# A third gate buffer and a new order of work around the state chunks of a delta-rule stage

## The chip, the cores and the metric

The kernel runs on one core of a Trainium2 chip. The metric is the device time of one execution in microseconds. Everything is float32; large matrix products are made of three products of rounded parts (high x high, high x low, low x high).

## What is computed

One decoder layer over 256 tokens of 2048 features: a half-step SwiGLU, a mixing layer (8 heads of latent attention beside 16 heads of an RWKV-7 delta rule), its output projection, a second half-step SwiGLU, and a gated per-layer embedding. The change concerns the delta rule alone:

```python
def step(state, inp):                  # for each of 16 heads, state 64 x 64
    r_t, w_t, k_t, v_t, kk_t, a_t = inp
    sa = jnp.einsum('bhvk,bhk->bhv', state, -kk_t)
    state = (state * w_t[:, :, None, :]
             + sa[..., None] * (kk_t * a_t)[:, :, None, :]
             + v_t[..., None] * k_t[:, :, None, :])
    return state, jnp.einsum('bhvk,bhk->bhv', state, r_t)
init = jnp.zeros((B, H, N, N))
...
o = (o - mu) * lax.rsqrt(var + GN_EPS)            # per head
o = o * ln_x_w + ln_x_b
o = (o + bonus) * g                                # bonus = sum(r*k*r_k) * v
```

## The kernel before

The 16 heads go through in four groups of four heads (`GROUPS`, r = 0 to 3), and a group's 256 tokens in four chunks of 64 (`NCHUNK`); two chunks make a tile of 128 tokens (t = 0, 1). For each group there are four steps.

1. **Front** (`front`, `with_decay`, on VectorE): keys, unit keys `kk`, learned keys `bb`, decayed copies `alpha`, `R_`, `B_`, `Kd`, the bonus. ScalarE makes the gates (`act_gates`), the last of them the output gate `gg`, from products that TensorE makes part by part (`pe_gates`). All of this is done for group r + 1 while group r is worked on. `gg` and `bonus` have two buffers each, used in turn.
2. **Scores and inverse** (`pe_scores`, `pe_inverse`, `inverse`): TensorE multiplies the turned keys, and a unit triangular matrix is inverted for each of 8 systems (4 heads x 2 tiles) in six levels. The first needs no products, the other five are n = 0 to 4. A level n is two rounds of products with a ScalarE copy into `Q` between and a VectorE copy into `XT` or `X` after, in halves of four systems. Levels 0 and 1 (`EARLY`) stand behind the scores, 2 to 4 (`LATER`) at the start of the group's turn. Level 3 is followed by AK times v (`pe_y`), which ScalarE copies into `Y` (`act_y`).
3. **State** (`pe_state`, `act_state`, `state`): products of alpha with X (copied to `W1T` by VectorE), then X with Y (copied to `U` by ScalarE), and a recurrence over the four chunks c. In chunk c, W1T times the state S is subtracted from U (VectorE, L1688), the queries read S (L1409), and Kd times v plus B_ times U (L1415, L1421) give the next S (VectorE, L1693 or L1698), with the decayed old state `SP` from ScalarE. S starts as a cleared buffer, which chunk 0 reads too. After chunk 1 TensorE turns (transposes) the next group's alpha into bank 3 (`turn`), after chunk 3 R_, B_ and Kd.
4. **Finish** (`out_centre`, `out_spread` on VectorE, `finish`, `gate_ahead` on GpSimd): centre, normalise, gate and add the bonus into `og`. TensorE transposes `og` (`pe_out`, into bank 1), ScalarE copies it to `xT_hi` (`act_out`), VectorE writes the rounding rest to `xT_lo` (`out_lo`). These three stand behind the inverse of the next group and ahead of its state step.

Each engine has its own queue, in the order of the program text; semaphores tie them together. `act_gates` waits, before it overwrites a `gg` buffer, for `o_ready` of the group that used it two groups before (L1488 to L1490). On ScalarE's queue that copy stands ahead of `Y` and of the copies of level 4. GpSimd's order is written out: `gate_ahead(0)`, `finish(0)`, `gate_ahead(1)`, `finish(1)` and so on. VectorE's work for the next group stands between the levels: key (L1569, L1580) behind level 2; own key and read (L1584, L1585, L1594) behind level 3; unit key and learned (L1588, L1589, L1569, L1592) behind level 4; read gain and read sum (L1569, L1598) ahead of chunk 0's S.

Of the kernel before, what the change touches and what calls it, by code (L numbers as in the profile page):

```python
# [16 lines left out]
P = 128  # L17
# [14 lines left out]
CHUNK = 64  # L32
# [85 lines left out]
def hybrid_layer(nc, table, w, out):  # L118
    where = constant_table()[1]
    ctx = ExitStack()  # L120
    with ctx:
# [1020 lines left out]
        def pool_rwkv(pool):  # L1142
# [5 lines left out]
            def gate_ahead(r):  # L1148

                b, k = bonus[:, r % 2, :, :], gg[:, r % 2, :, :]  # L1150
# [7 lines left out]
            def finish(r):  # L1158
# [5 lines left out]
                tt(og[:, :, :], oo[:, :, :], gg[:, r % 2, :, :], ALU.mult)  # L1164
# [40 lines left out]
        def sp_rwkv(sp):  # L1205
# [78 lines left out]
        def turn(pe, r, k):  # L1284
# [4 lines left out]
            if k == 3 and r:  # L1289
                pe.wait_ge(rs_copied, 2 * r)  # L1290
# [84 lines left out]
        def pe_state(pe, r, nxt):  # L1375

            pe.wait_ge(up_ready, 11 * r + 11)
# [61 lines left out]
        def pe_out(pe, r):  # L1439
            pe.wait_ge(o_ready, r + 1)  # L1440
            pe.wait_ge(ak_ready, 2 * min(r + 2, GROUPS))
            for pr in range(2):
                for t in range(TT):
                    ins = nc.tensor.transpose(PS[:, 1, (2 * pr + t) * P:(2 * pr + t + 1) * P], og[:, t, pr * P:(pr + 1) * P], ident)
# [7 lines left out]
        def pe_rwkv(pe):  # L1452
# [20 lines left out]
        def act_gates(act, r, part):  # L1473
# [22 lines left out]
        def act_scores(act, r, before):  # L1496
# [4 lines left out]
            act.wait_ge(bonus_ready, r + 1)  # L1501
# [513 lines left out]
```

## Time and profile before

| | |
|---|---|
| median of 3 runs | 2067.5 us (2067.19 to 2068.78) |
| the profiled execution's own time | 2067.66 us |
| its span | 2065.8 us |
| TensorE (PE) busy | 2024.1 us, 98% |
| VectorE (DVE) busy | 1155.3 us, 56% |
| ScalarE (ACT) busy | 859.6 us, 42% |
| GpSimd (POOL) busy | 148.0 us, 7% |
| DMA moved | 373.62 MB, 181 GB/s on the mean |

The delta-rule stage takes from about 997 us to 1139.5 us of the span. Times in the trace are microseconds from the span's start; a row has the start, the duration, the engine, the line and the operation, and in square brackets the time for which the engine had been idle and what released it. A busy TensorE is not TensorE at its peak. PEclk is the clock granted to TensorE, in parts of the full 2.4 GHz.

### The profile page before, as it was taken

Reading aid. Unit: us, or ns where it says so; the run is one execution under the profiler, and the core shown is the slowest. Engines: PE = TensorE matmul, PEld = TensorE weight load, DVE = VectorE, ACT = ScalarE, POOL = GpSimd, SP = SyncE. Lnnn points to the kernel's source line nnn. Section 1 sums busy time; section 2 is a strip of 40 time slices with the busy share of each in tenths; the row PEclk is TensorE's granted clock in tenths of the full one; section 3 lists DMA queues with packets and bytes.
Section 4 is the critical chain, followed back from the end, with each engine's and each line's share of the span. In section 5 each row is a group of like instructions: output and inputs, shape, how many; then the busy total and the mean of one; then the engine's idle time right before and its main releaser. Section 6 shows DMA issues by size and latency. Waiting matters only on the chain.

```text
span 2065.8 us, 27651 instructions
## 1 busy us (share of the span) xinstructions
PE 2024.1 (98%) x11448; PEld 1690.1 (82%) x11448; DVE 1155.3 (56%) x1027; ACT 859.6 (42%) x829; POOL 148.0 (7%) x117
## 2 busy tenths in 40 slices
PE   8999999999999999999887999999999999999999
PEld 6888888888888889888776888888888888888887
DVE  4455545555455565756877545555554555545564
ACT  6333333343343356854333345433333433333353
POOL 0000000000000000345324100000000000000000
PEclk9999999999999999999999999999999999999999
DMA  7565555655555546666312465656556555556554
GB/s 260 184 199 187 185 195 188 191 188 189 190 196 185 189 152 218 205 194 212 105 34 69 148 191 183 196 183 196 189 184 194 191 187 189 193 187 199 183 184 143
DMA packets 190049, 373.62 MB, mean 181 GB/s; under 512 B 7110, under 2 KB 16962, under 8 KB 189980
## 3 DMA queue, kind: packets, MB, share of 16 engines
q1 hardware_dynamic: 186300, 361.47, 54.3%
q0 software_dynamic: 3680, 11.15, 1.8%
q8 instruction: 53, 0.87, 0.2%
q14 instruction: 16, 0.13, 0.0%
HBM read 363.94 MB, written 5.52 MB: 179 GB/s over the span
## 4 chain that ended last, share of the span: by engine, by line
PE 92%; DVE 5%; issue 1%; POOL 0%; DMA 0%; ACT 0%; SPq 0%; DVEq 0%; POOLq 0%; ACTq 0%
PE PS L358 29%; PE PS L360 29%; PE PS L359 29%; PE PS L415 1%; PE PS L379 1%; DVE X L1645 0%; DVE wlo L344 0%; PE PS L1329 0%; DMA x_resid<-in_x 0%; DVE XT L1658 0%; DVE tmn L1569 0%; DVE AB L1631 0%; DVE AK L1631 0%; DVE U L1688 0%; DVE kk L1569 0%
## 5 line engine op out<-in xcount | busy, mean ns | idle before, releaser
L344 DVE TENSOR_TENSOR wlo<-raw,whi 128x2048 fp32r<-128x2048 f32 (+1 forms) x338 | 775.5, 2294 | 763.3 <-PE PS L360 758.0
L335 ACT ACTIVATE whi<-raw 128x2048 fp32r<-128x2048 f32 (+1 forms) x338 | 642.9, 1903 | 989.8 <-PE PS L360 985.8
L358 PE MATMUL PS<-whi,xT_hi 128*128 128x512 f32 (+2 forms) x1936 | 753.6, 389 | 0.0
L360 PE MATMUL PS<-whi,xT_lo 128*128 128x512 f32 (+2 forms) x1936 | 749.0, 387 | 0.0
L359 PE MATMUL PS<-wlo,xT_hi 128*128 128x512 f32 (+2 forms) x1936 | 748.5, 387 | 0.0
L360 PEld LDWEIGHTS PS<-whi,xT_lo 128*128 128x128 f32 x1936 | 363.8, 188 | 73.1
L358 PEld LDWEIGHTS PS<-whi,xT_hi 128*128 128x128 f32 x1936 | 364.0, 188 | 71.7 <-issue 0.4
L359 PEld LDWEIGHTS PS<-wlo,xT_hi 128*128 128x128 f32 x1936 | 364.1, 188 | 71.5
L358 PE MATMUL PS<-whi,hT_hi 128*128 128x512 f32 x680 | 265.2, 390 | 0.1
L360 PE MATMUL PS<-whi,hT_lo 128*128 128x512 f32 x680 | 264.9, 390 | 0.0
L359 PE MATMUL PS<-wlo,hT_hi 128*128 128x512 f32 x680 | 264.9, 390 | 0.0
L358 PEld LDWEIGHTS PS<-whi,hT_hi 128*128 128x128 f32 x680 | 127.7, 188 | 26.7 <-issue 0.4
L360 PEld LDWEIGHTS PS<-whi,hT_lo 128*128 128x128 f32 x680 | 127.7, 188 | 26.4
L359 PEld LDWEIGHTS PS<-wlo,hT_hi 128*128 128x128 f32 x680 | 127.8, 188 | 26.3
L550 DVE SCALAR_TENSOR_TENSOR x_resid<-PS,x_resid 128x512 f32<-128x512 f32 x184 | 118.1, 683 | 51.0 <-PE PS L360 51.0
L820 POOL TENSOR_TENSOR rstd<-rstd,con 128x2 f32<-128x2 f32 x6 | 6.3, 1044 | 1611.2 <-DVE rstd L815 1611.2
L397 DVE SCALAR_TENSOR_TENSOR xT_lo<-PS,gains,xT_hi 128x256 fp32r<-128x256 f32 x64 | 26.6, 478 | 28.8 <-ACT xT_hi L388 28.8
L388 ACT ACTIVATE xT_hi<-PS,gains 128x256 fp32r<-128x256 f32 x64 | 25.3, 476 | 38.7 <-PE PS L379 34.3
L1329 PE MATMUL PS<-XT,AB 64*64 64x64 f32 x640 | 26.7, 228 | 6.8 <-DVE XT L1645 4.3
L1329 PEld LDWEIGHTS PS<-XT,AB 64*64 64x64 f32 x640 | 22.2, 139 | 11.5 <-DVE XT L1658 5.3
L535 DVE SCALAR_TENSOR_TENSOR h<-PS,rstd,silu_g 128x512 f32<-128x512 f32 x44 | 30.9, 743 | 0.0
L541 DVE TENSOR_TENSOR hT_lo<-PS,hT_hi 128x1024 fp32r<-128x1024 f32 x20 | 24.5, 1225 | 10.1 <-ACT hT_hi L484 10.1
(329 smaller groups left out, 1106.8 us busy)
## 6 DMA issues: line engine op xcount, KB each, us to landing
raw<-in_w_gate SPq DMA_DIRECT2D x88, 1024.0 KB, 5.2
raw<-in_w_up SPq DMA_DIRECT2D x88, 1024.0 KB, 5.2
raw<-in_w_down SPq DMA_DIRECT2D x88, 1024.0 KB, 5.1
raw<-in_w_in SPq DMA_DIRECT2D x28, 1024.0 KB, 5.6
raw<-in_w_out SPq DMA_DIRECT2D x16, 1024.0 KB, 5.1
raw<-in_w_ple_gate SPq DMA_DIRECT2D x16, 1024.0 KB, 5.0
raw<-in_w_q_b SPq DMA_DIRECT2D x3, 1024.0 KB, 5.3
z_scratch<-zst POOLq DMA_DIRECT2D x6, 512.0 KB, 3.3
```

The source lines that it names most:

```text
L335: nc.scalar.activation(whi[:, n % WHI, 0:wd], raw[:, n % RAW, 0:wd], ACT.Copy).then_inc(hi_ready, 1)
L344: nc.vector.tensor_tensor(wlo[:, n % WLO, 0:wd], raw[:, n % RAW, 0:wd], f32(whi[:, n % WHI, 0:wd]), ALU.subtract).then_inc(lo_ready, 1)
L358: nc.tensor.matmul(acc, a, whi[:, n % WHI, c], start=st, stop=False)
L359: nc.tensor.matmul(acc, a, wlo[:, n % WLO, c], start=False, stop=False)
L360: ins = nc.tensor.matmul(acc, b, whi[:, n % WHI, c], start=False, stop=en)
L379: ins = nc.tensor.transpose(PS[:, turn_bank(k, u), j * SEQ + t * P:j * SEQ + (t + 1) * P], x[:, t, (2 * u + j) * P:(2 * u + j + 1) * P], i ...
L388: ins = nc.scalar.activation(xT_hi[:, kt, :], PS[:, turn_bank(k, u), j * SEQ:(j + 1) * SEQ], ACT.Copy, scale=gains[:, 16 * k + kt:16 * k + ...
L397: ins = nc.vector.scalar_tensor_tensor(xT_lo[:, kt, :], PS[:, turn_bank(k, u), j * SEQ:(j + 1) * SEQ], gains[:, 16 * k + kt:16 * k + kt + ...
L535: ins = nc.vector.scalar_tensor_tensor(h[:, t, :], PS[:, 2 + t, :], rstd[:, 4 * f + t:4 * f + t + 1], silu_g[:, t, :], ALU.mult, ALU.mult)
L541: nc.vector.tensor_tensor((dst or hT_lo)[:, :, :].rearrange("p (b j) s -> p b (j s)", b=2), PS[:, b:b + 2, :], f32((hi or hT_hi)[:, :, :]) ...
L550: ins = nc.vector.scalar_tensor_tensor(x[:, t, j * COLS:(j + 1) * COLS], PS[:, b + t, :], factor, x[:, t, j * COLS:(j + 1) * COLS], ALU.mu ...
L1329: ins = nc.tensor.matmul(PS[half(c), bank, out_col:out_col + CHUNK], a[half(c), s, a_cols], b[half(c)], start=start, stop=stop)
```

## The change

- `gg` gets a third buffer; group r uses buffer r % 3, and the copy into it waits for the output of group r - 3.
- In the state step the products of X with Y come first, one tile at a time, each with its own semaphore step, and ScalarE copies U tile by tile. The products of alpha with X follow.
- S isn't cleared. Chunk 0 reads no state. The output of chunk 0 is taken by ScalarE from bank 6 alone (one more copy of 64 rows, counted in `rs_copied`), and what is added to the reads covers the second half of tile 0 and all of tile 1.
- `pe_out` stands behind chunk 0, `act_out` and `out_lo` in chunk 1, and they use bank 3 instead of 1. The turn of the next alpha, in bank 3 too, waits for `heads_out`.
- `front(nxt, "read sum")` comes behind the S of chunk 0.
- ScalarE initialises X ahead of the copy of v; that copy waits for the group's loads instead of for `bonus_ready`, and the load queue waits for `bonus_ready` itself.

```diff
+        gg_third = sb("gg_third", [P, TT, 256])
+        def out_gate(r):
+            return (gg[:, 0, :, :], gg[:, 1, :, :], gg_third[:, :, :])[r % 3]
...
                 if r < GROUPS - 1:
                     sp.wait_ge(z_stored, 96)
                     sp.wait_ge(v_handed, r)
+                    sp.wait_ge(bonus_ready, r)
...
         def pe_state(pe, r, nxt):
-            pe.wait_ge(up_ready, 11 * r + 11)
+            pe.wait_ge(y_ready, r + 1)
+            for t in range(TT):
+                pe.wait_ge(up_ready, 11 * r + 10 + t)
+                for s, _, pr, par in systems(4 * t, 4 * t + 4):
+                    ins = by_chunks(6 + t, s, head(t, pr, par)[1].start, X, half(0), Y[:, s, :])
+                ins.then_inc(w2_done, 1)
             for t in range(TT):
...
             ins.then_inc(w1_done, 1)
-            pe.wait_ge(y_ready, r + 1)
-            for s, t, pr, par in systems():
-                sy, cc = head(t, pr, par)
-                ins = by_chunks(6 + t, sy, cc.start, X, half(0), Y[:, sy, :])
-            ins.then_inc(w2_done, 1)
-            pe.wait_ge(w1_ready, r + 1)
-            pe.wait_ge(s_ready, 4 * r + 1)
             if nxt is not None:
                 pe.wait_ge(exps_ready, 5 * nxt + 5)
-            if r:
-                pe.wait_ge(heads_out, 2 + r)
             for c in range(NCHUNK):
...
                 if c:
-                    pe.wait_ge(s_ready, 4 * r + c + 1)
+                    pe.wait_ge(w1_ready, r + 1)
+                    pe.wait_ge(s_ready, 3 * r + c)
...
-                    pe.wait_ge(rs_copied, 2 * r + 1)
-                for pr, par, _, cc in pairs:
+                    pe.wait_ge(rs_copied, 3 * r + 1)
+                for pr, par, _, cc in pairs if c else ():
...
+                if c == 0 and r:
+                    pe_out(pe, r - 1)
                 if nxt is not None and c == 1:
+                    if r:
+                        pe.wait_ge(heads_out, 2 + r)
                     turn(pe, nxt, 0)
...
         def pe_out(pe, r):
             pe.wait_ge(o_ready, r + 1)
-            pe.wait_ge(ak_ready, 2 * min(r + 2, GROUPS))
...
-                    ins = nc.tensor.transpose(PS[:, 1, ...
+                    ins = nc.tensor.transpose(PS[:, 3, ...
...
-                if r >= 2:
-                    act.wait_ge(o_ready, r - 1)
-                nc.scalar.activation(gg[:, r % 2, :, :], tiles(two), ACT.Copy).then_inc(exps_ready, 1)
+                if r >= 3:
+                    act.wait_ge(o_ready, r - 2)
+                nc.scalar.activation(out_gate(r), tiles(two), ACT.Copy).then_inc(exps_ready, 1)
...
-            act.wait_ge(bonus_ready, r + 1)
+            nc.scalar.activation(X[:, :, :], const("ident_chunk")..., ACT.Copy).then_inc(xinit, 1)
+            act.wait_ge(*loaded(r))
             nc.scalar.activation(vv[:, :, :], ZZ[r % 2][:, :, 2, :], ACT.Copy).then_inc(v_handed, 1)
-            nc.scalar.activation(X[:, :, :], const("ident_chunk")..., ACT.Copy).then_inc(xinit, 1)
...
         def act_state(act, r, nxt):
-            act.wait_ge(w2_done, r + 1)
             for t in range(TT):
+                act.wait_ge(w2_done, 2 * r + t + 1)
...
+                if c == 1 and r:
+                    act_out(act, r - 1)
+                if c == 3:
+                    act.wait_ge(ou_done, 2 * r + 1)
+                    nc.scalar.activation(oo[half(0), 0, :], PS[half(0), 6, 0:256], ACT.Copy).then_inc(rs_copied, 1)
...
             def state(r, nxt):
-                v.memset(S[:, :, :], 0.0).then_inc(s_ready, 1)
                 dve.wait_ge(w1_done, r + 1)
...
                     front(nxt, "read gain")
-                    front(nxt, "read sum")
...
+                    if c == 1 and r:
+                        out_lo(r - 1)
+                    if nxt is not None and c == 0:
+                        front(nxt, "read sum")
...
                 inverse(it, LATER, nxt, None)
-                if it:
-                    out_lo(it - 1)
                 state(it, nxt)
```

## Rows read from the trace of the kernel before

**Rows 1.** The page, part 4: share of the span on the last chain.

```profile
PE 92%; DVE 5%; issue 1%; POOL 0%; DMA 0%; ACT 0%; SPq 0%; DVEq 0%; POOLq 0%; ACTq 0%
```

**Rows 2.** Waits, 995 to 1160 us: total, times, longest (us).

```profile
ACT gg L1490 <- POOL og L1171: 12.3, 2, 6.2
```

**Rows 3.** Timeline of group 1, level 4: start, us, engine, operation, [idle before].

```profile
1046.03 1.13 PE L1275 MATMUL PS<-wl_a,lora_t 128*128 128x256 f32 x4
...
1050.96 1.59 POOL L1171 TENSOR_TENSOR og<-og,bonus 128x512 f32<-128x512 f32 x1
1051.46 1.63 DVE L1594 SCALAR_TENSOR_TENSOR tmn<-zz_a,k 128x512 f32<-128x512 f32 x1
1052.51 1.71 POOL L1070 TENSOR_TENSOR bonus<-bonus,lnc 128x512 f32<-128x512 f32 x1
1052.64 0.60 ACT L1490 ACTIVATE gg<-PS 128x512 f32<-128x512 f32 x1 [6.22 <-POOL og L1171]
...
1053.95 1.60 PE L1329 MATMUL PS<-X,Q 64*64 64x64 f32 x32 [3.85 <-ACT Q L1512]
1054.30 1.27 POOL L1070 TENSOR_TENSOR bonus<-bonus,gg 128x512 f32<-128x512 f32 x1
...
1054.83 0.30 DVE L1656 COPY_PREDICATED X<-con,PS 128x128 f32<-128x128 uint32 x1
...
1055.47 1.11 PE L1444 MATMUL PS<-con,og 128*128 128x128 f32 x4
1055.59 0.30 DVE L1656 COPY_PREDICATED X<-con,PS 128x128 f32<-128x128 uint32 x1 [0.46 <-issue]
...
1055.64 1.26 POOL L1156 TENSOR_TENSOR gg<-gg,lnc 128x512 f32<-128x512 f32 x1
1055.79 1.14 DVE L1588 TENSOR_SCALAR hsf<-hsf 128x8 f32<-128x8 f32 x1
...
1057.21 0.69 DVE L1569 TENSOR_TENSOR kk<-kk,hsf 128x512 f32<-128x512 f32 x1
...
1058.66 0.69 DVE L1730 TENSOR_TENSOR xT_lo<-PS,xT_hi 128x512 fp32r<-128x512 f32 x1
...
1059.41 0.63 DVE L1677 COPY W1T<-PS 128x512 f32<-128x512 f32 x1
```

**Rows 4.** Timeline of group 1, chunks 0 to 2.

```profile
1061.38 0.29 DVE L1693 TENSOR_TENSOR S<-PS,pc 128x128 f32<-128x128 f32 x1
...
1062.31 0.42 DVE L1688 TENSOR_TENSOR U<-U,PS 64x256 f32<-64x256 f32 x1
...
1063.28 0.48 DVE L1698 SCALAR_TENSOR_TENSOR S<-PS,pc,SP 128x64 f32<-128x64 f32 x2 [0.55 <-PE PS L1421]
...
1063.63 0.65 PE L1293 MATMUL PS<-con,alpha 128*128 128x128 f32 x4
...
1064.21 0.45 PE L1403 MATMUL PS<-S,W1T 64*64 64x64 f32 x8
...
1064.71 0.41 DVE L1688 TENSOR_TENSOR U<-U,PS 64x256 f32<-64x256 f32 x1 [0.35 <-PE PS L1403]
```

**Rows 5.** Timeline of group 2: VectorE's product behind level 3, and W1T.

```profile
1090.38 1.63 DVE L1594 SCALAR_TENSOR_TENSOR tmn<-zz_b,k 128x512 f32<-128x512 f32 x1
...
1098.32 0.63 DVE L1677 COPY W1T<-PS 128x512 f32<-128x512 f32 x1
```

**Rows 6.** Timeline of group 0: the same product, and the first copy into X.

```profile
1015.73 1.64 DVE L1594 SCALAR_TENSOR_TENSOR tmn<-zz_b,k 128x512 f32<-128x512 f32 x1
...
1017.42 0.29 DVE L1656 COPY_PREDICATED X<-con,PS 128x128 f32<-128x128 uint32 x1
```

**Rows 7.** Timeline of group 3: TensorE's products of chunk 1.

```profile
1133.91 0.45 PE L1403 MATMUL PS<-S,W1T 64*64 64x64 f32 x8
```

**Rows 8.** Windows: busy us of PE, PEld, DVE, ACT, POOL; PEclk; DMA share, GB/s.

```profile
1055.00:1057.00 2.00, 2.00 (x31) 1.55 (x32) 1.50 (x5) 0.38 (x1) 1.83 (x2) 0.50 0.00 0
1059.00:1062.00 3.00, 1.65 (x48) 1.51 (x50) 2.93 (x7) 0.72 (x4) 0.00 (x0) 1.00 0.14 39
```

More of the change, by code:

```diff
@@ L1148, in gate_ahead @@
             def gate_ahead(r):
-                b, k = bonus[:, r % 2, :, :], gg[:, r % 2, :, :]
+                b, k = bonus[:, r % 2, :, :], out_gate(r)
                 pool.wait_ge(exps_ready, 5 * r + 5)
@@ L1163, in finish @@
                     pool.wait_ge(heads_out, 2 + r)
-                tt(og[:, :, :], oo[:, :, :], gg[:, r % 2, :, :], ALU.mult)
+                tt(og[:, :, :], oo[:, :, :], out_gate(r), ALU.mult)
                 pool.wait_ge(out_var, r + 1)
@@ L1289, in turn @@
             if k == 3 and r:
-                pe.wait_ge(rs_copied, 2 * r)
+                pe.wait_ge(rs_copied, 3 * r)
             for pr in range(2):
@@ L1440, in pe_out @@
             pe.wait_ge(o_ready, r + 1)
-            pe.wait_ge(ak_ready, 2 * min(r + 2, GROUPS))
             for pr in range(2):
                 for t in range(TT):
-                    ins = nc.tensor.transpose(PS[:, 1, (2 * pr + t) * P:(2 * pr + t + 1) * P], og[:, t, pr * P:(pr + 1) * P], ident)
+                    ins = nc.tensor.transpose(PS[:, 3, (2 * pr + t) * P:(2 * pr + t + 1) * P], og[:, t, pr * P:(pr + 1) * P], ident)
             ins.then_inc(o_turned, 1)
@@ L1528, in act_state @@
                 if c < NCHUNK - 1:
-                    act.wait_ge(s_ready, 4 * r + c + 1)
+                    act.wait_ge(s_ready, 3 * r + c)
                     for pr in range(2):
@@ L1534, in act_state @@
                     act.wait_ge(rs_done, 2 * r + c // 2 + 1)
-                    nc.scalar.activation(oo[:, c // 2, :].rearrange("p (pr par n) -> p par pr n", pr=2, par=2),
-                                         PS[:, 1:3, (c // 2) * P:(c // 2 + 1) * P].rearrange("p b (pr n) -> p b pr n", pr=2),
+                    tokens = half(1) if c == 1 else slice(0, P)
+                    nc.scalar.activation(oo[tokens, c // 2, :].rearrange("p (pr par n) -> p par pr n", pr=2, par=2),
+                                         PS[tokens, 1:3, (c // 2) * P:(c // 2 + 1) * P].rearrange("p b (pr n) -> p b pr n", pr=2),
                                          ACT.Copy).then_inc(rs_copied, 1)
+                if c == 1 and r:
[3 more added lines that the diff above has]
+                    nc.scalar.activation(oo[half(0), 0, :], PS[half(0), 6, 0:256], ACT.Copy).then_inc(rs_copied, 1)
                 if nxt is not None and c == 1:
@@ L1542, in act_out @@
             act.wait_ge(o_turned, r + 1)
-            nc.scalar.activation(xT_hi[:, bass.ds(2 * r + HEADS, 2), :], PS[:, 1, :].rearrange("p (a s) -> p a s", a=2),
+            nc.scalar.activation(xT_hi[:, bass.ds(2 * r + HEADS, 2), :], PS[:, 3, :].rearrange("p (a s) -> p a s", a=2),
                                  ACT.Copy).then_inc(head_hi, 1)
@@ L1553, in act_rwkv @@
                 act_inverse(act, it, LATER)
-                if it:
-                    act_out(act, it - 1)
                 act_state(act, it, nxt)
@@ L1707, in add_inner @@
             def add_inner(r, t):
-                dve.wait_ge(rs_copied, 2 * r + t + 1)
+                dve.wait_ge(rs_copied, 3 * r + t + 1)
                 dve.wait_ge(ou_done, 2 * r + t + 1)
-                v.tensor_tensor(oo[:, t, :], oo[:, t, :], PS[:, 6 + t, 0:256], ALU.add).then_inc(ou_read, 1)
+                tokens = half(1) if t == 0 else slice(0, P)
+                v.tensor_tensor(oo[tokens, t, :], oo[tokens, t, :], PS[tokens, 6 + t, 0:256], ALU.add).then_inc(ou_read, 1)
             def out_centre(r):
                 dve.wait_ge(ou_read, 2 * r + 2)
+                dve.wait_ge(rs_copied, 3 * r + 3)
                 o_ = oo[:, :, :]
@@ L1729, in out_lo @@
                 dve.wait_ge(head_hi, 3 + r)
-                v.tensor_tensor(xT_lo[:, bass.ds(2 * r + HEADS, 2), :], PS[:, 1, :].rearrange("p (a s) -> p a s", a=2),
+                v.tensor_tensor(xT_lo[:, bass.ds(2 * r + HEADS, 2), :], PS[:, 3, :].rearrange("p (a s) -> p a s", a=2),
                                 f32(xT_hi[:, bass.ds(2 * r + HEADS, 2), :]), ALU.subtract).then_inc(heads_out, 1)
```

4 lines of the change are left out of this document (1 added, 3 removed).

## The prediction

> **What bounds the kernel now.** I read the chain that ended last first: it lies on TensorE for 92% of the span and on VectorE for 5% [rows 1]. The two feed-forward stages are therefore out of reach of this change; it touches only the delta-rule stage, from about 997 to 1139.5 us, where the chain hops between engines. The span is 2065.8 us, the profiled execution 2067.66 us, so 1.86 us lie around the span, and it stands 0.16 us above the median of 2067.5 us. What moves the end of the delta-rule stage moves the end of the program one to one, since the output projection starts right behind it and TensorE has no gap in it.
>
> Next I asked the waits of that stage. One concerns an engine that should be free: ScalarE waits 12.3 us in two cases to write `gg`, until GpSimd has finished the output of the group before [rows 2]. In group 1 (heads 4 to 7) the gate product ends at 1047.16, but its copy starts only at 1052.64, behind the GpSimd addition that ends at 1052.55. Behind the copy on ScalarE's queue stand `Y` and the last two copies of `Q`, and TensorE's last level of the inverse starts at 1053.95 after 3.85 us of idling [rows 3].
>
> What would end next? VectorE has its own work for the next group between the last two levels: it ends at 1051.46 + 1.63 = 1053.09, and the first copy into `X` comes at 1054.83 [rows 3]. So of the 3.85 us only 1.74 us are seen on VectorE. In group 2 the same work ends at 92.01 (I leave out the 1000) and W1T comes at 98.32 [rows 5]. Group 0, where there is no such wait, shows what is left when it is gone: VectorE's work ends at 1017.37 and the copy into `X` follows at 1017.42, without idling [rows 6].
>
> **Part 1, the third buffer.** Groups 2 and 3 write buffers 2 and 0; the wait for a finished output becomes one for the group before that, long done. The copy of `gg` (0.60 us) runs at about 1047.2, in ScalarE's idle time. `Y` waits for its products, not for it. In group 1 the last products are then through by about 1051.5, and the copies into `X` come as in group 0, 0.05 us behind VectorE: 1053.13 for the first instead of 1054.83, and some 0.2 us later the second, instead of 1055.59. The second gains 2.25 us, because the transposes of the finished outputs (1.11 us on TensorE, [rows 3]), which now stand between, are also gone from there.
>
> That is not yet the gain. Behind the copies VectorE normalises the key (clamp, reciprocal, product `kk`), then makes `bb`. At that time GpSimd prepares the next gate: 1052.51 to 1054.22, 1054.30 to 1055.57, 1055.64 to 1056.90. Before, `kk` started at 1057.21, with GpSimd done. The rows show what happens when they meet: the clamp of eight numbers took 1.14 us and ended 0.03 us behind GpSimd's operation; the product L1594 took 1.63 us, ending 0.54 us behind GpSimd's (1052.55), and the GpSimd operation that started behind it ran until 1.13 us after the VectorE operation that held it [rows 3]. So they alternate. GpSimd's times hang on the key's variance and on VectorE's earlier work, neither of which moves. Laid out: the clamp starts about 1053.5 and ends 1054.25; the clamp's end to `kk` is 0.28 us (1056.93 to 1057.21), so `kk` is due at 1054.53, and GpSimd has started its second operation 0.23 us before. `kk` ends at 1055.57 + 0.54 = 1056.11, GpSimd's third at 1056.11 + 1.13 = 1057.24, and `bb` at 57.24 + 0.54 = 1057.78. W1T takes the place of the split of the old output (L1730, 1058.66) right behind `bb`, since that split and the clearing of S (together 0.75 us, up to 1059.41) have left: with 0.04 us between, as elsewhere on VectorE's queue, 1057.82 instead of 1059.41, 1.59 us earlier [rows 3]. Group 2 has the same order: 92.01 + (57.82 - 53.09) = 96.74 against 98.32, 1.58 us earlier [rows 5].
>
> A rule of the Trainium skill speaks against the change here. SBUF — State Buffer, "Who interferes with whom", says that the port pair that VectorE and GpSimd share is an exclusive lock, so that whoever comes second waits for the whole operation. By it `kk` and `bb` pay in full, as the rows say; if the two only shared a bandwidth, they would keep near 0.7 us and the gain would be that of the first rival.
>
> **Part 2, first chunk and order of products.** VectorE is busy from W1T at 1059.41 to the first U subtraction at 1062.31: W1T, read gain, read sum, S (1061.38), alpha, U [rows 3, 4]. Moving the read sum behind S only makes S earlier; U still stands behind both. The clearing of S gives less than 0.1 us per group (0.75 us less L1730's 0.69 us and the steps between), counted above for groups 1 and 2; I take 0.1 us for group 0. Putting Y's products first and dropping eight reads (eight such products take 0.45 us in a row of their own [rows 4], by estimate 0.35 us of issue) shortens an engine that idles here: after its products it waits for W1T and S. Cost 0 in groups 0 to 2; hidden under VectorE's front work. The added copy of `oo` has half of the columns of `gg`'s, whose copy took 0.60 us [rows 3]; on ScalarE's queue it stands ahead of BT, and the turn of Kd now waits for it: between 0, when VectorE's copies behind the chunks are later anyway, and 0.3 us a group. I take 0, since VectorE's queue has the next queries, the inner sum and the bonus ahead of what reads Kd. The X initialisation ahead of vv, and vv's new wait, are in ScalarE's idle time too: 0. The added wait on the load queue is on something issued before the loads: 0.
>
> **Part 3, the old output inside the chunks.** Transposes and ScalarE's copy (0.60 us) are placed in idle time after chunk 0; the move out of the inverse is counted in part 1. The split on VectorE is not free: it comes after S of chunk 1, and TensorE must not turn alpha before it, because both use bank 3. Behind that wait on TensorE stand the turn and the products of chunk 2. Now S ends at 1063.76, the turn starts before that, at 1063.63, W1T times S at 1064.21, and U follows at 1064.71 [rows 4]. Afterwards the split ends 0.60 us behind S's end, the turn starts 0.05 us later, and the products follow by the old 0.58 us, at S + 1.23 instead of S + 0.45: 0.78 us lost in each of groups 1 and 2. So these gain 1.59 - 0.78 = 0.81 us and 1.58 - 0.78 = 0.80 us. Group 0 has no old output: 0.1 us.
>
> **Group 3** has no next group, so TensorE bounds its first chunks: it runs without idling up to the products of chunk 1 at 1133.91 [rows 7]. It loses eight reads (-0.35 us), starts by estimate 0.2 us earlier with the first tile, and gets the old output's transposes, which hold what follows by 0.58 us like the turn of alpha (1063.63 to 1064.21 [rows 4]) and before stood in a gap of the inverse. So the products of chunk 1 are where they were. VectorE's split adds 0.1 us at most behind S. I take 0, bounds -0.4 and +0.4.
>
> **Sum:** 0.1 + 0.81 + 0.80 + 0 = 1.7 us, against the profiled execution 2067.66 - 1.7 = 2066.0 us, against the median **2065.8 us**. The bounds of group 3 (0.4 us either way), the turn of Kd (up to 0.9 us in all) and some 0.3 us of scatter of a median give 2065.1 to 2067.4 around it.
>
> **The rivals.** *A: GpSimd does not hold `kk` and `bb`.* If GpSimd gives way (it need start only 0.23 us later), they end at 54.53 + 1.41 = 55.94 instead of 57.78, and groups 1 and 2 gain 1.84 us more each: 2065.8 - 3.7 = 2062.1 us. Against it stand the product L1594 in three groups (1.63, 1.63, 1.64 us [rows 3, 5, 6], where a product of that size without GpSimd took 0.69 us) and the clamp. Chance 0.10.
>
> *B, on the slow side: TensorE's clock falls before chunk 1.* After the change it finishes the first chunk's work near 1056, by estimate (products from 1053.5, some 2.5 us of them), and waits for S until 1059.4, over 3 us. After 3.85 us of idling the granted clock was 0.50 from 1055 to 1057, the 1.2 GHz level, and 1.00 again from 1059 [rows 8]. At that level four transposes took 1.11 us [rows 3] against 0.65 us [rows 4]: 0.46 us for the turn, and by estimate 0.2 us for each of the three groups of eight products on the chain, together 1.05 us. It decides as soon as it costs more than the 0.80 us gained per group: then 0.25 us are lost in each, and with group 0's 0.1 us the time is 2067.5 + 0.5 - 0.1 = 2067.9 us, with group 3 at its upper bound 2068.3 us. Chance 0.10. TensorE: Matmul & The Clock Gate, Part 1, of the Trainium skill also makes the clock depend on how busy the engine has been, and would let it fall in this gap.
>
> *C: the turn of alpha does not hold chunk 2* (S's own end hides more of the split than I think): 2 x 0.78 us come back, 2064.2 us. Chance 0.10. *D: the third buffer only exposes another wait*, say ScalarE's copies held by `Y`, and the change does nothing: 2067.4 us. The idle time ahead of 1053.95 names only Q. Chance 0.05.
>
> **How the numbers follow.** Forecast 0.65, A 0.10, B 0.10, C 0.10, D 0.05. The range leaves out A and most of B: 2063.4 to 2067.9 us. A measurement of this kernel can tell about 0.2%, 4.1 us. Only A and a combination of A with C pass that: 0.09 faster. Slower by 4.1 us would need more than all bounds together: 0.02. Same: 0.89.
>
> **What would show it.** Right: `gg` copied near its product's end in all groups, no GpSimd wait ahead of it; X copied 0.05 us behind VectorE's product in groups 1 and 2; `kk` and `bb` at about 1.6 us instead of 0.69 us in those two; TensorE's turn of alpha released by VectorE's split. Wrong: `kk` at 0.69 us with X early (A), a granted clock near half in the chunks (B), products of chunk 2 at S + 0.45 us (C).

## The result, and the profile after

The changed kernel takes 2072.6 us (median of 20 runs, 2069.4 to 2077.7), the kernel before 2067.5 us (20 runs of its own beside them, 2065.5 to 2070.8). The ratio is 1.0022, with an interval of 1.0016 to 1.0028. That is 5.1 us slower by the medians and 3.3 to 5.8 us by the interval, where 1.7 us faster was forecast.

The profiled execution of after is one of its quickest: 2069.37 us, with a span of 2067.6 us. That is 3.2 us under the median, and the mean granted clock goes with it. Each run has such a mean over its span. Of the 20 runs of after, six at 0.994 took 2069.4 to 2069.7 us, those at 0.991 and 0.992 took 2071.4 to 2074.3 us, and one at 0.988 took 2077.7 us; a line through all has 1.26 us for each 0.001. The mean of the 20 is 0.9921. The kernel before has 0.9955 as its mean over the 86 runs made beside the experiments, 51 of them at 0.996 exactly; a line through those has 0.80 us for each 0.001. The two profiled spans are 2067.6 and 2065.8 us, so the trace below shows 1.8 us of the loss.

The page of after, its span and the first line of its chain that ended last (to be held against [rows 1]):

```profile
span 2067.6 us, 27601 instructions
PE 92%; DVE 5%; issue 1%; DMA 0%; ACT 0%; SPq 0%; DVEq 0%
```

The shares are those of before. The waits of the delta-rule stage (waiting engine and its instruction, releaser; us in total, times, longest):

```profile
PEld PS L1299 <- DVE xT_lo L1743: 1.0, 2, 0.5
ACT gg_third L1494 <- PE PS L1281: 0.8, 1, 0.8
PE PS L1406 <- DVE S L1700: 5.9, 3, 2.9
```

The 12.3 us behind GpSimd of [rows 2] are gone: the gate's copy waits 0.8 us for its own product. The new wait of the turn of alpha for the split (first line) is there, twice. The last line is TensorE waiting for the first S: 1.65 us in group 0, 2.91 in group 1 and 1.40 in group 2.

Group 1, the timeline (start, us, engine, line, operation, out<-in, count, and in brackets the idle time before it with its releaser), to be held against [rows 3]. In all timelines rows between those shown are left out, also where no dots stand.

```profile
1046.77 0.60 ACT L1494 ACTIVATE gg_third<-PS 128x512 f32<-128x512 f32 x1 [0.77 <-PE PS L1281]
...
1050.93 1.63 DVE L1603 SCALAR_TENSOR_TENSOR tmn<-zz_a,k 128x512 f32<-128x512 f32 x1
1052.61 0.30 DVE L1665 COPY_PREDICATED X<-con,PS 128x128 f32<-128x128 uint32 x1
...
1053.77 1.27 POOL L1075 TENSOR_TENSOR bonus<-bonus,gg 128x512 f32<-128x512 f32 x1
1054.00 1.60 DVE L1578 TENSOR_TENSOR kk<-kk,hsf 128x512 f32<-128x512 f32 x1
1055.12 1.59 POOL L1161 TENSOR_TENSOR gg<-gg,lnc 128x512 f32<-128x512 f32 x1
1055.63 1.63 DVE L1601 SCALAR_TENSOR_TENSOR bb<-aa,kk 128x512 f32<-128x512 f32 x1
1057.30 0.69 DVE L1685 COPY W1T<-PS 128x512 f32<-128x512 f32 x1
```

`gg` is copied 5.9 us earlier, X follows VectorE's own work by 0.05 us (1050.93 + 1.63 = 1052.56, then 1052.61), `kk` and `bb` take 1.60 and 1.63 us beside GpSimd, and W1T follows `bb` by 0.04 us. From X to W1T it is 4.69 us, and the prediction had 57.82 - 53.13 = 4.69. All steps of Part 1 are here as forecast.

The chunks of the same group, to be held against [rows 4], and the windows of the stretch (columns as in [rows 8]):

```profile
1058.62 0.29 DVE L1700 TENSOR_TENSOR S<-PS,pc 128x128 f32<-128x128 f32 x1
1059.06 0.61 PE L1406 MATMUL PS<-S,W1T 64*64 64x64 f32 x8 [2.91 <-DVE S L1700]
1060.26 0.42 DVE L1695 TENSOR_TENSOR U<-U,PS 64x256 f32<-64x256 f32 x1
1061.87 0.68 DVE L1743 TENSOR_TENSOR xT_lo<-PS,xT_hi 128x512 fp32r<-128x512 f32 x1
1062.61 1.11 PE L1299 MATMUL PS<-con,alpha 128*128 128x128 f32 x4 [0.33 <-DVE xT_lo L1743]
1063.65 0.69 PE L1406 MATMUL PS<-S,W1T 64*64 64x64 f32 x8
1064.39 0.41 DVE L1695 TENSOR_TENSOR U<-U,PS 64x256 f32<-64x256 f32 x1 [1.24 <-PE PS L1406]
```

```profile
1058.00:1060.00 2.00, 0.94 (x22) 0.97 (x22) 1.93 (x4) 0.59 (x2) 0.00 (x0) 0.80 0.58 126
1060.00:1062.00 2.00, 1.79 (x32) 1.60 (x28) 1.17 (x5) 0.97 (x2) 0.00 (x0) 0.50 0.00 0
1062.00:1064.00 2.00, 1.68 (x13) 1.16 (x13) 1.15 (x2) 0.24 (x1) 0.00 (x0) 0.50 0.00 0
1064.00:1066.00 2.00, 2.00 (x45) 2.00 (x43) 0.74 (x3) 0.83 (x3) 0.00 (x0) 0.50 0.03 8
```

Here the forecast breaks. TensorE idles 2.91 us for S, its granted clock falls to 0.50 (1.2 GHz) soon after it has begun again and stays there up to 1066. The turn takes 1.11 us where it took 0.65, the products with S 0.61 and 0.69 us where a row of before had 0.45. From the first U subtraction to the second it is 4.13 us; before it was 2.40 (1062.31 to 1064.71). Group 2 has the same 4.13 us, although TensorE idles only 1.40 us for its S: the half clock comes there from about 1100 to 1107, after another one from 1093.3 to 1096.7.

Read off in this way for all four groups (starts on VectorE's rows, in us; the last two columns lead to the next group, and the masked copies are those that start its inverse, without products):

| kernel | X to W1T | W1T to first U | first to second U | second to third U | third U to the masked copies | those to the next X |
|---|---|---|---|---|---|---|
| before | 3.0, 4.6, 4.2, 1.3 | 2.9, 2.9, 2.9, 2.7 | 2.40, 2.40, 2.40, 2.0 | 2.68, 2.67, 2.68, 2.0 | 4.46, 4.47, 4.46 | 22.0, 22.3, 19.6 |
| after | 2.8, 4.7, 4.7, 2.1 | 3.0, 3.0, 3.0, 1.9 | 2.41, 4.13, 4.13, 2.1 | 2.67, 2.99, 2.99, 2.1 | 4.71, 4.71, 5.25 | 20.2, 20.2, 19.7 |

### The profile page after: what moved, and what is told of

Same layout as the page of the kernel before. It is cut to its first block, busy times and chain, and to the rows that moved or that the text cites. A ratio compares the mean times of both kernels' runs of the same rounds, so it can differ in the third digit from the quotient of the medians.

```text
span 2067.6 us, 27601 instructions
## 1 busy us (share of the span) xinstructions
PE 2024.4 (98%) x11416; PEld 1691.1 (82%) x11416; DVE 1159.2 (56%) x1023; ACT 861.7 (42%) x833; POOL 151.1 (7%) x117
## 4 chain that ended last, share of the span: by engine, by line
PE 92%; DVE 5%; issue 1%; DMA 0%; ACT 0%; SPq 0%; DVEq 0%
PE PS L363 29%; PE PS L365 29%; PE PS L364 29%; PE PS L420 1%; PE PS L384 1%; DVE X L1654 0%; DVE wlo L349 0%; DVE XT L1667 0%; DMA x_resid<-in_x 0%; DVE kk L1578 0%; PE PS L1335 0%; PE PS L1299 0%; DVE AB L1640 0%; DVE AK L1640 0%; DVE k L1594 0%
```

## Experiments

My theory after this reading: the path got shorter as forecast, and TensorE's clock took back more than that. Its rivals: that the third buffer by itself does the harm, through the collisions on VectorE; that the new wait of the turn does it; and that the idle time before chunk 1 alone decides, so that whatever breaks it helps. Kernels sent together ran on one chip beside runs of the kernel before, whose medians there were 2067.4 (1 to 4), 2067.8 (5 to 8) and 2067.6 us (9 to 12). The kernel after ran only beside its own 20 runs of before, so a difference to it below crosses sets, and it is clear only where the intervals don't overlap. All medians and clocks (mean over the runs) at a glance:

| run | kernel | us | ratio to before, interval | clock |
|---|---|---|---|---|
| | before | 2067.5 | 1 | 0.9955 |
| | after | 2072.6 | 1.0022, 1.0016 to 1.0028 | 0.9921 |
| 1 | after, idle gap of chunk 0 filled | 2068.9 | 1.0011, 1.0001 to 1.0020 | 0.9962 |
| 2 | after, two gaps filled | 2067.7 | 1.0003, 0.9994 to 1.0012 | 0.9974 |
| 3 | before, third buffer alone | 2068.2 | 1.0003, 0.9994 to 1.0012 | 0.9950 |
| 4 | after with two buffers | 2071.5 | 1.0020, 1.0011 to 1.0029 | 0.9937 |
| 5 | before, gaps filled | 2066.2 | 0.9995, 0.9986 to 1.0004 | 0.9984 |
| 6 | after, split ahead of S | 2071.1 | 1.0015, 1.0006 to 1.0024 | 0.9933 |
| 7 | after, GpSimd's gate first | 2064.4 | 0.9982, 0.9973 to 0.9991 | 0.9957 |
| 8 | after, 6 and 7 together, read sum later | 2059.0 | 0.9957, 0.9943 to 0.9971 | 0.9970 |
| 9 | 8, gaps filled | 2062.7 | 0.9977, 0.9967 to 0.9986 | 0.9983 |
| 10 | before, GpSimd's gate first | 2065.9 | 0.9992, 0.9983 to 1.0001 | 0.9965 |
| 11 | 2 with products as filler | 2068.4 | 1.0007, 0.9998 to 1.0016 | 0.9971 |
| 12 | after, chunk 0 held until W1T | 2077.0 | 1.0041, 1.0028 to 1.0055 | 0.9902 |

### 1 and 2: TensorE kept busy in its gaps

Transposes of the identity into an unused part of a bank, placed where TensorE idles. Run 1 has them between chunks 0 and 1 (12 in group 0, 24 in groups 1 and 2):

```diff
+        def turn_idle(pe, n):
+            for _ in range(n):
+                nc.tensor.transpose(PS[:, 1, 256:384], ident, ident)
...
                     pe_out(pe, r - 1)
+                if c == 0 and nxt is not None:
+                    turn_idle(pe, 24 if r else 12)
```

Run 2 adds the gap behind the inverse:

```diff
         def pe_state(pe, r, nxt):
+            turn_idle(pe, (8, 18, 18, 16)[r])
             pe.wait_ge(y_ready, r + 1)
```

> The changed kernel with TensorE kept busy by transposes of the identity (results unused) in the idle time between chunk 0 and chunk 1: 24 in groups 1 and 2, 12 in group 0. Theory CLOCK (the loss is TensorE's clock falling in the recurrence over chunks, because it has idled before): the granted clock stays 1.00 through chunks 1 and 2 of groups 1 and 2, the chunk 2 subtraction from U comes 1.2 to 1.3 us behind chunk 1's state update instead of 2.4 us, and the median falls from 2072.6 to 2067 or below. Rival ORDER (the moved split, its wait and the other new waits cost the time, and the clock falls where nobody waits): the median stays within 1 us of 2072.6.

> As the run before, and 8, 18, 18 and 16 transposes more in groups 0 to 3 in the idle time before the products of X with Y. CLOCK: the stage's low stretches all go but the one ahead of group 3, the median is 2065.8, my sum before the result (1.7 us under the kernel before), at most 2067. ORDER: 2072.6, or more by what the fillers hold up.

They gave 2068.9 and 2067.7 us: 3.7 and 4.9 us under after, for work that computes nothing. The interval of run 2 lies clear of that of after, that of run 1 overlaps it a little, and neither kernel came down to the 2067 us and the 2065.8 to 2067 us expected of them. The profiled executions differ less from that of after: 2067.71 and 2067.70 us, 1.7 us under it. The timeline of group 1 in run 1, and its windows:

```profile
1055.88 2.78 PE L1384 MATMUL PS<-con 128*128 128x128 f32 x24
1060.17 0.42 DVE L1702 TENSOR_TENSOR U<-U,PS 64x256 f32<-64x256 f32 x1
...
1062.27 0.66 PE L1299 MATMUL PS<-con,alpha 128*128 128x128 f32 x4 [0.71 <-DVE xT_lo L1750]
1062.86 0.45 PE L1411 MATMUL PS<-S,W1T 64*64 64x64 f32 x8
1063.35 0.41 DVE L1702 TENSOR_TENSOR U<-U,PS 64x256 f32<-64x256 f32 x1 [0.54 <-PE PS L1411]
```

```profile
1060.00:1062.00 2.00, 0.91 (x24) 0.78 (x24) 1.42 (x5) 0.66 (x2) 0.00 (x0) 1.00 0.04 8
1062.00:1064.00 2.00, 1.67 (x35) 1.37 (x37) 1.23 (x3) 1.04 (x3) 0.00 (x0) 1.00 0.00 0
```

The clock is 1.00 in the chunks; first to second U is 3.18 us where after has 4.13, second to third 2.67 where it has 2.99. So the half clock costs 0.95 + 0.32 = 1.27 us a group here. The remaining 0.78 us over the 2.40 of before are the turn's wait for the split. In group 2 of this execution the clock is at half from about 1092.4 to 1095.8 instead, and the fillers then hold up W1T to the first U (3.43 us instead of 2.97). The clock over the whole run rose from 0.9921 to 0.9962 and 0.9974; at 1.26 us for each 0.001 that is 5.1 and 6.7 us, of which 3.7 and 4.9 arrive.

### 3 and 4: the third buffer alone, the order alone

Run 3 is the kernel before with the third buffer and nothing else; run 4 is the kernel after with the two buffers of before.

```diff
-                nc.scalar.activation(gg[:, r % 2, :, :], tiles(two), ACT.Copy).then_inc(exps_ready, 1)
+                if r >= 3:
+                    act.wait_ge(o_ready, r - 2)
+                nc.scalar.activation(out_gate(r), tiles(two), ACT.Copy).then_inc(exps_ready, 1)
```

```diff
-            return (gg[:, 0, :, :], gg[:, 1, :, :], gg_third[:, :, :])[r % 3]
+            return gg[:, r % 2, :, :]
...
-                if r >= 3:
-                    act.wait_ge(o_ready, r - 2)
+                if r >= 2:
+                    act.wait_ge(o_ready, r - 1)
```

> The kernel before with the third buffer alone. By my rows, kk and bb collide with GpSimd as in the changed kernel, the old split stays on VectorE before W1T, the turn of alpha doesn't wait: 0.8 us gained in each of groups 1 and 2 at full clock, 2065.9. CLOCK leaves it open where the low stretches fall: 2065.5 to 2069. ORDER: 2065.9, since nothing of the order is changed.

> The changed kernel with two gate buffers and the old wait (the new order alone). ScalarE waits again for GpSimd, 12 us in two cases, and TensorE idles about 3.9 us in groups 1 and 2. ORDER: this carries the whole loss and the buffer's gain is missing, 2074 or more. CLOCK: the low stretches sit where they sat in the kernel before and the two order costs and gains cancel, 2067 to 2070.

The buffer alone changes nothing that can be told (2068.2 us, clock 0.9950), where 2065.9 us was expected. Its gain is there: in groups 1 and 2 the first copy into X follows the masked copies after 20.3 and 20.2 us instead of 22.0 and 22.3. It goes again behind that: X to W1T takes 5.43 us in both (4.58 and 4.19 in before), W1T to the first U 3.46 and 3.45 (2.90), and in group 1 first to second U 3.17 (2.40). From 1054 to 1062 the clock is 0.50 there, with two microseconds in which TensorE does nothing. The order alone has most of the loss, 2071.5 us, between what the two theories expected of it (up to 2070, and 2074 or more). Its waits show that the buffer's gain isn't in it (same columns as above):

```profile
ACT gg L1494 <- POOL og L1176: 12.2, 2, 6.1
```

So of the change's two halves only the order of work shows a loss by itself. But one view of run 4 warns against tying it to one place. A window of group 0's inverse, where TensorE's program is that of before, then the same window of before:

```profile
1010.00:1012.00 2.00, 2.00 (x44) 2.00 (x42) 1.41 (x7) 0.45 (x1) 0.02 (x1) 0.50 0.64 262
```

```profile
1010.00:1012.00 2.00, 2.00 (x65) 1.94 (x64) 1.97 (x3) 1.14 (x2) 1.59 (x2) 1.00 0.00 0
```

The kernel after, whose program for group 0 is that of run 4, has 1.00 in this window too. The rows ahead of it show what differs, first in run 4, then in after:

```profile
1000.00 2.34 POOL L1075 TENSOR_TENSOR pvst<-pvst,zst 128x1024 f32<-128x1024 f32 x1 [4.24 <-DMA pvst<-zst]
1000.20 3.23 DVE L1025 TENSOR_TENSOR xT_lo<-ho,xT_hi 128x1024 fp32r<-128x1024 f32 x1
...
1003.69 1.61 PE L1335 MATMUL PS<-XT,AB 64*64 64x64 f32 x26 [1.86 <-DVE XT L1667]
```

```profile
1000.32 1.18 DVE L1025 TENSOR_TENSOR xT_lo<-ho,xT_hi 128x1024 fp32r<-128x1024 f32 x1
1000.43 3.28 POOL L1075 TENSOR_TENSOR pvst<-pvst,zst 128x1024 f32<-128x1024 f32 x1 [4.38 <-DMA pvst<-zst]
```

It is a race. GpSimd's operation starts when a transfer has landed, VectorE's split (of the attention heads' output) when its queue gets there. In run 4 GpSimd is first by 0.20 us, the split takes 3.23 us instead of 1.18, TensorE idles 1.86 us, the half clock follows from 1004 to 1014, and the first copy into X comes at 1021.42 instead of 1016.82. In after VectorE is first by 0.11 us, in before by 1.33 us. Of the 14 profiled executions GpSimd won in two, those of runs 4 and 7, and these two are 3.0 and 3.3 us above the medians of their kernels. How often after loses this race in the executions that have no trace isn't known. One loss is worth 4 to 4.6 us (an estimate from these starts), more than the 3.2 us between after's profile and its median, so this is an untested rival for that part of the loss.

### 5: the same filler in the kernel before

```diff
+                if last and r in (1, 2):
+                    turn_idle(pe, 28)
...
+            if nxt is not None:
+                pe.wait_ge(exps_ready, 5 * nxt + 5)
+                turn_idle(pe, 10, 2)
             pe.wait_ge(w1_ready, r + 1)
```

> The kernel before, with 28 transposes of the identity in the 3.9 us in which TensorE waits for the last copies of Q in groups 1 and 2, and 10 in each group with a next one between the products of X with Y and chunk 0. CLOCK (a lower clock costs in both kernels, but in the kernel before it falls where TensorE's work is partly hidden): 0.5 to 1.5 us under the kernel before. If the clock costs the kernel before nothing: 2067.4, unchanged.

It gave 2066.2 us, ratio 0.9995 (0.9986 to 1.0004), with the highest clock of all, 0.9984. So filling is worth 1.5 us by the medians in before, from 0.8 us lost to 2.9 us gained by the interval, where it was worth 3.7 and 4.9 us in after. The windows around the turn of [rows 3], now at full clock:

```profile
1054.00:1056.00 2.00, 2.00 (x70) 1.76 (x68) 1.61 (x7) 0.60 (x1) 1.92 (x2) 1.00 0.03 8
1056.00:1058.00 2.00, 1.95 (x35) 1.65 (x30) 1.93 (x3) 0.66 (x2) 0.39 (x1) 1.00 0.15 25
```

Here the two profiled executions differ. Before had its half clock from about 1054.4 to 1057.8, where VectorE's `kk`, `bb` and split mostly set the pace and TensorE's slower products lay beside them: with the filler W1T follows the masked copies after 26.14 us instead of 26.58, so 0.4 us of it were on the path. After has it from about 1059.2 to 1066, in the chunks, whose products are on the path, for 1.27 us.

### 6: the turn's wait taken away

The split goes ahead of the S update of chunk 1, and ScalarE's copy ahead of the chunks, so that the turn of alpha finds it done.

```diff
                                         ALU.subtract).then_inc(u_ready, 1)
+                    if c == 1 and r:
+                        out_lo(r - 1)
                     if c < NCHUNK - 1:
...
-                    if c == 1 and r:
-                        out_lo(r - 1)
```

> The changed kernel with the split of the old output (and ScalarE's copy ahead of it) moved between chunk 1's subtraction from U and its state update, so that the turn of alpha finds it done. By the step on the turn's wait (0.78 us lost per group in 1 and 2, 0.14 us of it left because the split is 0.14 us longer than the idle time there): the row of the turn has no wait for the split, the subtraction of chunk 2 follows S's end by 0.95 us at full clock, and the median falls by 1.3 us, to 2071.3. If the wait was hidden: unchanged, 2072.6.

```profile
1062.05 0.42 DVE L1695 TENSOR_TENSOR U<-U,PS 64x256 f32<-64x256 f32 x1
1062.50 0.69 DVE L1743 TENSOR_TENSOR xT_lo<-PS,xT_hi 128x512 fp32r<-128x512 f32 x1
1063.37 0.66 PE L1299 MATMUL PS<-con,alpha 128*128 128x128 f32 x4
1064.45 0.41 DVE L1695 TENSOR_TENSOR U<-U,PS 64x256 f32<-64x256 f32 x1 [0.28 <-PE PS L1406]
```

The chunks of group 1 run at full clock in this execution, and first to second U is 1064.45 - 1062.05 = 2.40 us, the value of before. Against the 3.18 of run 1 the wait is worth 0.78 us, the number of Part 3. The median fell by 1.5 us (2071.1 us), about 2 x 0.78, as expected, but the intervals overlap, and the clock rose a little too (0.9933), so the median alone doesn't show it. Group 0 of this execution speaks against the last rival, that the idle time before chunk 1 alone decides: it is 1.64 us, the half clock follows, and first to second U takes 3.65 us; after has 1.65 us there, keeps full clock and takes 2.41.

### 7 and 10: GpSimd's order

GpSimd takes the next group's gate ahead of finishing the output of this one, so that its three operations are over before VectorE's `kk` and `bb`. Run 7 has it in after, run 10 in before.

```diff
+            gate_ahead(0)
             for r in range(GROUPS):
-                gate_ahead(r)
+                if r < GROUPS - 1:
+                    gate_ahead(r + 1)
                 finish(r)
```

> The changed kernel with GpSimd's gate preparation of the next group ahead of the finish of this one, so that it runs about 10 us earlier and nobody of GpSimd's long operations lies beside kk and bb. By the step on the collisions: kk and bb take 0.69 us each instead of 1.60 and 1.63, the clamp 0.17 instead of 0.7, in groups 1 and 2, W1T comes 2.3 to 2.4 us earlier, and the median falls by 4 us or more, to 2068 or below, if the clock stays as it is. If the collisions were hidden behind TensorE: unchanged, 2072.6.

> The kernel before with GpSimd's new order alone. In it kk and bb lay behind GpSimd's operations, only the clamp waited (1.14 and 0.76 us instead of 0.17): by the rows 1.5 us gained, 2066.0. If the GpSimd order were worth its 8 us in any kernel: 2060.

Run 7: 2064.4 us, 8.2 us under after and 3.3 under before. Its rows of group 1, the gate's operation that now runs some 17 us earlier (1051.98 in after), then VectorE:

```profile
1035.06 1.27 POOL L1075 TENSOR_TENSOR bonus<-bonus,lnc 128x512 f32<-128x512 f32 x1 [15.36 <-DVE bonus L1613]
...
1058.58 0.69 DVE L1580 TENSOR_TENSOR kk<-kk,hsf 128x512 f32<-128x512 f32 x1
1059.31 0.69 DVE L1603 SCALAR_TENSOR_TENSOR bb<-aa,kk 128x512 f32<-128x512 f32 x1
1061.13 0.69 DVE L1687 COPY W1T<-PS 128x512 f32<-128x512 f32 x1 [1.13 <-PE PS L1396]
```

`kk` and `bb` are at 0.69 us each: 1.85 us less in each of groups 1 and 2, as rival A had it. In the profiled execution the clock is at 0.50 there and W1T waits 1.13 us for TensorE, so not all of it shows in this trace. Run 8 has the same order of GpSimd and full clock there, and X to W1T takes 2.30 us instead of 4.69 in groups 1 and 2, with the clamp at 0.16 instead of 0.71 us: 4.8 us in all. A split of weights in group 3 takes 2.29 us instead of 3.02 in run 7. The way from the masked copies to X is 0.2 us longer twice (20.43 instead of 20.20). That makes 5.1 us by the rows, where 4 or more were expected; the other 3 or so go with the higher clock (0.9957 against 0.9921) and with the race of run 4, and no run tells these two apart. The same edit in before is worth 1.7 us by the medians (2065.9, as expected), but its interval holds 1 (0.9983 to 1.0001). There `kk` already started behind GpSimd [rows 3].

### 8 and 9: both moves, and both with fillers

Run 8 has the edits of runs 6 and 7, and the read sum of the next group behind the U subtraction of chunk 2 instead of in chunk 0:

```diff
+                    if nxt is not None and c == 2:
+                        front(nxt, "read sum")
...
-                    if nxt is not None and c == 0:
-                        front(nxt, "read sum")
```

Run 9 adds the fillers of run 2.

> The changed kernel with the GpSimd order of the run before, the early split, and the read sum between chunk 2's subtraction and its state update instead of behind chunk 0's state. No fillers. Sum of the steps: -4.6 -1.3 -1.1 us against the changed kernel, 2065.6, under the kernel before by 1.8 us; with a clock that stays up for the shorter gaps (below 1 us before chunk 1), 2063.

> The kernel with GpSimd's new order, the early split and the late read sum, with the transposes of the identity in both gaps (24 before chunk 1 are more than its gap now holds: it is about 1 us, they take 2.6). If fillers only pay where TensorE idles, they hold up chunk 1 here: slower than the run without them (2059.0) by 1.5 us or more per group in groups 1 and 2, 2062 or more. If the clock still costs more than that: below 2059.

Run 8 is the best: 2059.0 us (2058.3 to 2060.2), ratio 0.9957 with an interval of 0.9943 to 0.9971, 8.8 us under before and 13.6 under after. The steps had been expected to give 2065.6 us, or 2063 with a clock that stays up.

```profile
1053.28 0.29 DVE L1667 COPY_PREDICATED X<-con,PS 128x128 f32<-128x128 uint32 x1
1054.13 0.69 DVE L1580 TENSOR_TENSOR kk<-kk,hsf 128x512 f32<-128x512 f32 x1
...
1055.58 0.69 DVE L1687 COPY W1T<-PS 128x512 f32<-128x512 f32 x1
...
1057.34 0.45 PE L1408 MATMUL PS<-S,W1T 64*64 64x64 f32 x8 [0.52 <-DVE S L1706]
1057.82 0.42 DVE L1697 TENSOR_TENSOR U<-U,PS 64x256 f32<-64x256 f32 x1
...
1060.23 0.41 DVE L1697 TENSOR_TENSOR U<-U,PS 64x256 f32<-64x256 f32 x1 [0.28 <-PE PS L1408]
```

X to W1T is 2.3 us (after: 4.7), W1T to the first U 2.24 (3.0), first to second U 2.41 (4.13). The idle time before the first products with S is 0.52 us instead of 2.91, and the clock of the window behind is 1.00:

```profile
1060.00:1062.00 2.00, 1.66 (x51) 1.41 (x47) 1.74 (x5) 0.91 (x3) 0.00 (x0) 1.00 0.04 8
```

Run 9, 2062.7 us, is 3.7 us slower than run 8 though its clock is higher (0.9983 against 0.9970). With the gap gone the fillers themselves stand on the path: W1T to the first U takes 4.29 us in groups 1 and 2. In these runs fillers pay only where TensorE waits anyway.

### 11 and 12: what kind of work, and where the gap lies

Run 11 is run 2 with products of 256 columns, a quarter as many, instead of transposes; they keep TensorE busy for as long (2.76 us in group 1, against 2.78). Run 12 is after with chunk 0 held on TensorE until W1T is ready, so that the gap before chunk 1 becomes short and the one before chunk 0 long.

```diff
-            for _ in range(n):
-                nc.tensor.transpose(PS[:, 1, 256:384], ident, ident)
+            for _ in range(n // 4):
+                nc.tensor.matmul(PS[:, 1, 256:512], ident, con[:, 0:256], start=True, stop=True)
```

```diff
+            pe.wait_ge(w1_ready, r + 1)
             for c in range(NCHUNK):
...
-                    pe.wait_ge(w1_ready, r + 1)
```

> The changed kernel filled in both gaps as in the second run, but with a quarter as many products of the identity with 256 columns of constants instead of transposes of 128. If what kind of work fills the gap matters for the clock: fewer low stretches, mean granted clock above the 0.996 of the transposes and 1 us or more below 2067.7. If not: 2067.7 within 1 us.

> The changed kernel in which chunk 0 waits on TensorE for W1T, as it did before, so that TensorE's idle time in front of chunk 1 is cut in two (before chunk 0 and after it) instead of lying in one piece of 2.9 us. S comes at most 0.3 us later per group. If the one long gap makes the clock fall: a median 1 to 3 us below 2072.6. If only the sum of idle time counts: 2072.6 to 2073.6.

Run 11: 2068.4 us, clock 0.9971, next to run 2's 2067.7 and 0.9974. The kind of work makes no difference that can be told, as expected. Run 12: 2077.0 us with the lowest clock, 0.9902. Neither of the two times expected of it came (1 to 3 us below 2072.6, or 2072.6 to 2073.6).

```profile
1059.89 0.69 DVE L1685 COPY W1T<-PS 128x512 f32<-128x512 f32 x1
1060.73 0.69 PE L1418 MATMUL PS<-vv,Kd 64*64 64x64 f32 x8 [3.46 <-DVE W1T L1685]
...
1062.59 1.11 PE L1450 MATMUL PS<-con,og 128*128 128x128 f32 x4
1064.38 0.42 DVE L1695 TENSOR_TENSOR U<-U,PS 64x256 f32<-64x256 f32 x1 [0.78 <-PE PS L1406]
```

The gap was not cut, it moved and grew to 3.46 us, and now chunk 0's products and the old output's transposes (1.11 us, so at the lower clock) stand behind it on the path: W1T to the first U takes 4.49 us instead of 2.97. The loss against after is 4.4 us. The length of the gap and what stands behind it changed together, so this run doesn't tell the two apart.

## Why the prediction was wrong, point by point

- *Part 1 held.* `gg` early, X 0.05 us behind VectorE, `kk` and `bb` at 1.60 and 1.63 us because GpSimd holds them, X to W1T 4.69 us as laid out. In runs 7 and 8, where GpSimd is done before, both take 0.69 us. The alternation on which Part 1 rested is thus shown. By SBUF — State Buffer of the Trainium skill, "Who interferes with whom", it is an exclusive lock; the runs agree (0.69 us alone, 1.60 and 1.63 us beside GpSimd).
- *Part 3 held in mechanism and size.* The turn of alpha is released by the split, and that costs 0.78 us: 3.18 against 2.40 us at full clock (runs 1 and 6).
- *Part 2 was a little off.* Behind the third U, the way to the masked copies for the next group takes 4.71 us instead of 4.46 in groups 0 and 1, at full clock too, and 5.06 (run 1, full clock) to 5.25 (after, partly at half clock) in group 2. For the later copy of `oo` I had taken 0 with a bound of 0.3 us a group. VectorE's steps there are further apart, and no wait that the trace names explains it; whether `oo` is the cause stays open.
- *The sum at full clock.* Up to the third U the forecast was close. I take the steps of before from its trace, and for after those of run 1 in groups 0 and 1 and of run 2 in group 2, whose clock is full in these chunks. Group 0: 2.97 + 2.90 + 2.40 + 2.68 = 10.95 us before, 2.83 + 2.96 + 2.41 + 2.67 = 10.87 after: 0.1 gained (0.1 forecast). Group 1, from the masked copies on: 22.00 + 4.58 + 2.90 + 2.40 + 2.67 = 34.55 us before, 20.20 + 4.70 + 2.96 + 3.18 + 2.67 = 33.71 after: 0.84 gained (0.81). Group 2: 22.28 + 4.19 + 2.90 + 2.40 + 2.68 = 34.45 before, 20.21 + 4.71 + 2.96 + 3.19 + 2.67 = 33.74 after: 0.71 gained (0.80). Behind the third U 0.25 + 0.25 + 0.6 = 1.1 us are lost, and group 3 loses 0.2 with the way to it (19.58 + 1.32 + 2.74 + 2.00 + 1.99 against 19.69 + 2.10 + 1.86 + 2.08 + 2.08), inside its bounds of 0.4. So some 0.4 us were left of the 1.7.
- *The step that failed: the sum has no term for TensorE's clock.* Part 2 put the earlier products at "Cost 0 in groups 0 to 2" because they shorten an engine that idles, and the sum took every product behind that idle time at full clock. The runs showed 2.91 us of idle time in group 1, a clock of 0.50 in the chunks behind it, and 1.27 us lost in each of groups 1 and 2 (4.13 and 2.99 us against 3.18 and 2.67), more than the 0.81 and 0.80 gained. From the first copy into X of group 0 to the third U of group 3 before takes 120.97 us and after 123.34; after starts this 0.6 us sooner, and 2.4 - 0.6 is the 1.8 us between the spans. Without 2 x 1.27 us the profiled after would be 0.7 us quicker than before.
- *Rival B was the case, and it was mis-sized.* I had put it at a chance of 0.10 and at 2067.9 to 2068.3 us. Its place was right, and its price near: 1.05 us forecast, 1.27 measured. Priced was one such event in each of two groups, 2.5 us as measured, and the median has lost 5.1. The other 3.2 us lie in executions whose traces aren't kept, with a lower mean clock than the profiled one (six of 20 runs were as quick as it). The mean over the runs, 0.9921 against 0.9955, gives 4.3 us at the 1.26 us for each 0.001 of after's runs and 2.7 us at the 0.80 of before's, so neither rate is a price. Whether those 3.2 us are more half clock in the chunks, or the race of run 4 with the half clock that it brings, or both, stays open.
- *The probability was the deeper fault.* [rows 8] had shown the clock at half behind a gap in this very stage. I read it as something the change removes, and did not ask where it goes when the path behind the gap is one that waits for TensorE. TensorE: Matmul & The Clock Gate, Part 1, of the Trainium skill, which I had cited for B, makes the clock hang on recent activity; the rows agree (0.50 behind 2.91 us of idle time), and it would have borne more than 0.10.
- *What isn't settled.* That filling the gaps raises the clock is shown (runs 1, 2, 5, 11), and that it brings the time back in after (2 clear of the noise, 11 at its edge). That the order alone carries a loss is shown too (3, 4). Why the new order meets a half clock more often than the old is not: it would take traces of several executions of each, the race at 1000 us taken away, and no run here takes the new order apart into its steps.

## What to carry to other kernels

In a stage whose chain hops between engines, moving work off a wait also moves where TensorE's half clock falls; ask of each gap that stays what stands behind it, and prefer it where another engine sets the pace. When a step is advanced, look at what a neighbour that can hold it up is doing at the new time (GpSimd beside VectorE: 1.60 instead of 0.69 us): reordering GpSimd was worth 8.2 us with the change, and 1.7 us without it, which the noise doesn't let one tell from nothing. And compare many runs with their clocks, for a single profile is one draw: that of after was 3.2 us better than its median. Two operations that hold each other up started 0.11 us apart in it, and which of them is first is worth some 4 us.

## What the runs showed of the hardware

- One program took 2069.4 to 2077.7 us over 20 runs, in step with its mean granted clock (0.994 to 0.988). The kernel before spread over 2065.5 to 2070.8 us.
- The granted clock was 0.50 in windows of 2 us in which TensorE was 84 to 100% busy, with 64x64 products and four transposes (1060 to 1066 of after), behind a gap of 2.9 us. Behind gaps of 1.64 and 1.65 us at the same place of the program it fell to 0.50 in one execution (run 6, group 0) and stayed at 1.00 in another (after).
- Filling gaps with useless transposes or products raised the mean clock from 0.992 to 0.997, and from 0.9955 to 0.998 in before, and gave 4.9 us by the medians, and 1.5 us in before, there within the noise; where no gap was left it cost 3.7 us (run 9 against 8).
- Elementwise operations of VectorE beside GpSimd took 1.60 and 1.63 us instead of 0.69, one by one in turn, and GpSimd's 1.59 instead of 1.27.
- Two operations that meet by chance: with GpSimd first by 0.20 us VectorE's 1024-column split took 3.23 us (run 4), with VectorE first by 0.11 us it took 1.18 (after), and the first copy into X came 4.6 us later than there.
